# Block products in the gate stage of a three-layer float32 kernel: what the change does to the time

## The reference, cut to what matters

```python
hn = _rmsnorm(h, norm_g[i])
u = hn @ w_in[i]                       # projections, convolution branch, banded attention
...
h = h + jnp.concatenate([ya, yb], axis=-1) @ w_out[i]
e = _rmsnorm(p[i] @ w_pe[i], pe_g[i])  # 512 x 256 by 256 x 2048
h = h + e * jax.nn.sigmoid(h @ w_pg[i])
```

## Time and profile before

| | us |
|---|---|
| median of three runs (2524.76 to 2526.66) | 2524.79 |
| profiled execution | 2524.99 |
| its span | 2523.2 |
| TensorE busy in the span | 2515.8 |
| first layer's gate stage, first to last matmul (716.8 to 890.9) | 174.1 |

### The profile page before, as it was taken

How to read it: one execution, slowest core, us unless ns; L and a number is a source line. 1 busy time by engine, 2 the same in 40 slices (tenths; PEclk the granted TensorE clock), 3 DMA queues, 4 the chain that set the end, 5 groups by cost and what they waited for, 6 DMA issues and landing times.

```text
span 2523.2 us, 40982 instructions
## 1 busy us (share of the span) xinstructions
PE 2515.8 (100%) x15264; PEld 2130.5 (84%) x15264; DVE 1549.4 (61%) x2510; ACT 1066.7 (42%) x1618; POOL 1324.5 (52%) x1668
## 2 busy tenths in 40 slices
PE   9999999999999999999999999999999999999999
PEld 7888888889988888888878899888888888899887
DVE  7977766575462387777665745634654655955722
ACT  6212365643462342223655434634322656545421
POOL 6555554443355555555454434555666776534554
PEclk9999999999999999999999999999999999999999
DMA  7322243248733333223432487233322323388322
GB/s 251 114 92 99 97 123 113 91 144 210 165 108 125 116 118 101 98 94 101 120 114 95 162 188 171 92 133 114 112 98 94 101 92 100 98 188 241 101 95 105
DMA packets 95424, 313.56 MB, mean 124 GB/s; under 512 B 9456, under 2 KB 25584, under 8 KB 92208
## 3 DMA queue, kind: packets, MB, share of 16 engines
q1 hardware_dynamic: 75264, 268.45, 31.6%
q0 software_dynamic: 10368, 37.75, 8.6%
q10 hardware_dynamic: 9648, 5.36, 1.0%
HBM read 297.86 MB, written 16.81 MB: 125 GB/s over the span
## 4 chain that ended last, share of the span: by engine, by line
PE 99%; DMA 0%; ACT 0%; DVE 0%; issue 0%; SPq 0%; POOL 0%; DVEq 0%; ACTq 0%
PE acc L2070 18%; PE acc L2071 18%; PE acc L2072 17%; PE sc L2071 6%; PE sc L2070 6%; PE sc L2072 6%; PE sc L2340 2%; PE sc L2341 2%; PE sc L2342 2%; PE acc L2340 1%; PE acc L2341 1%; PE acc L2342 1%; PE acc L2094 1%; PE sc L2094 1%; PE sc L2096 1%; PE sc L2100 1%
## 5 line engine op out<-in xcount | busy, mean ns | idle before, releaser
L792 POOL TENSOR_TENSOR WL<-raw,WH 128x256 fp32r<-128x256 f32 x1504 | 1195.0, 827 | 907.6 <-ACT WH L852 907.3
L2070 PE MATMUL acc<-XH,WH 128*128 128x512 f32 x1936 | 756.4, 391 | 0.1
L2071 PE MATMUL acc<-XL,WH 128*128 128x512 f32 x1936 | 753.7, 389 | 0.0
L2072 PE MATMUL acc<-XH,WL 128*128 128x512 f32 x1936 | 753.3, 389 | 0.0
L852 ACT ACTIVATE WH<-raw 128x1024 fp32r<-128x1024 f32 x378 | 398.9, 1058 | 795.2 <-PE acc L2072 538.6
L2070 PEld LDWEIGHTS acc<-XH,WH 128*128 128x128 f32 x1936 | 363.4, 188 | 80.5 <-issue 4.9
L2072 PEld LDWEIGHTS acc<-XH,WL 128*128 128x128 f32 x1936 | 363.5, 188 | 76.0
L2071 PEld LDWEIGHTS acc<-XL,WH 128*128 128x128 f32 x1936 | 363.5, 188 | 74.3
L2070 PE MATMUL sc<-XH,WH 128*128 128x512 f32 x640 | 249.0, 389 | 0.0
L2071 PE MATMUL sc<-XL,WH 128*128 128x512 f32 x640 | 249.0, 389 | 0.0
L2072 PE MATMUL sc<-XH,WL 128*128 128x512 f32 x640 | 249.0, 389 | 0.0
(11 more groups left out here) (425 smaller groups left out, 4408.3 us busy)
## 6 DMA issues: line engine op xcount, KB each, us to landing
raw<-in_w SPq DMA_DIRECT2D x416, 512.0 KB, 3.3
raw<-in_w POOLq DMA_DIRECT2D x54, 512.0 KB, 6.2
a<-in_w POOLq DMA_DIRECT2D x18, 512.0 KB, 5.9
a<-in_w SPq DMA_DIRECT2D x16, 512.0 KB, 7.6
h_spill<-H SPq DMA_DIRECT2D x8, 1024.0 KB, 6.1
H<-h_spill SPq DMA_DIRECT2D x8, 1024.0 KB, 8.2
a<-bias_band SPq DMA_DIRECT2D x16, 384.0 KB, 3.7
H<-in_x SPq DMA_DIRECT2D x5, 1024.0 KB, 7.6
```

The source lines that it names most:

```text
L792: part = pool.tensor_tensor(WL[:, c], raw[:, c], WH[:, c].bitcast(F), ALU.subtract)
L2070: pe.matmul(bank, WH[:, c], xh, start=first, stop=False)
L2071: pe.matmul(bank, WH[:, c], xl, start=False, stop=False)
L2072: return pe.matmul(bank, WL[:, c], xh, start=False, stop=last)
```

## The change

The gate stage of both layers now runs its 16 tiles as P_PLAIN = 6 plain tiles (0 to 3, 14 and 15) and P_PAIRS = 5 pairs of tiles (4 to 13) as block products, 35 in each layer, in the order `P_STEPS`.

- **Plain tiles** alternate between the two banks G; `halve` is gone, ScalarE takes the tanh from the bank (or from T for the tiles of pairs) with scale 0.5.
- **Sums of h** for the block products are made at the stage's start: `sum_adds`, `third_add`, `sum_highs`, `third_high`, `sum_lows`, `third_low`, and `sums_of(4)` during the last plain unit. They need the room of Y, so e is stored to DRAM (`e_spill`, four parts), and comes back tile by tile (`e_load`) into `acc` and `rs`, the last two tiles into Y.
- **Weights of the block products** have five places: the four slots of `raw` and the fourth slot of WL (`wa2`). Low parts therefore rotate through three slots of WL (`p_low_slot`); high parts keep four. The chain p1, p5, p6, p4 of a pair uses one of three places `wa`, and p2, p3, p7 share one of two places `wd`.
- **Low parts** of p2 and p7 (all but the first, nine in a layer) are made by GpSimd, the others by VectorE, at most two products ahead (`block_lows(j + 2)` in turn j; three ahead in the stages of before).
- **Results** go to T (`block_outs`); a finished tile is then gated, squared and summed, in turns set by `g_done(n)`.
- **Stores** of h: tiles 0 to 3 go out before the block products, the other twelve, 256 KB each, during the next stage's first units.
- At the next stage TensorE starts its pair of tiles after the products that held its banks.

```diff
+P_PLAIN = 6
+P_PAIRS = 5
+P_STEPS = (
+    ("p2", 0), ("p1", 0), ("p5", 0), ("p3", 0), ("p1", 1), ("p6", 0), ("p2", 1), ("p7", 0), ("p5", 1), ("p4", 0), ("p3", 1), ("p6", 1),
+    ("p1", 2), ("p7", 1), ("p2", 2), ("p5", 2), ("p4", 1), ("p3", 2), ("p6", 2),
+    ("p1", 3), ("p7", 2), ("p2", 3), ("p4", 2), ("p5", 3), ("p1", 4),
+    ("p3", 3), ("p6", 3), ("p5", 4), ("p3", 4), ("p7", 3), ("p6", 4), ("p4", 3), ("p7", 4), ("p2", 4), ("p4", 4))
+def p_slot(j):
+    return (j + (j >= 14)) % RING
+def p_low_slot(j):
+    return RING - 1 if j == P_N - 1 else (j + 2) % (RING - 1)
+def p_place(kind, q):
+    if kind in ("p1", "p5", "p6", "p4"):
+        return "wa%d" % ((q + 1) % 3)
+    return "wd%d" % ((q + 1) % 2 if (kind, q) == ("p2", P_PAIRS - 1) else q % 2)
...
@@ GpSimd
+                for j, (kind, q) in enumerate(P_STEPS):
+                    name = p_place(kind, q)
+                    if j in P_SIDE:
+                        pool.wait_ge(fast_high, fast_base(ly) + j + 1)
+                        pool.wait_ge(*p_wl_free(ly, j))
+                        for k in range(LOW_PARTS):
...
+                            part = pool.tensor_tensor(WL[:, to], P_PLACE[name][:, lo:hi], WH[:, high].bitcast(F), ALU.subtract)
+                        part.then_inc(side_low, 1)
+                    if p_next(j) is not None and not p_loads(p_next(j)):
+                        pool.wait_ge(*p_low_made(ly, j))
+                        pool.dma_start(P_PLACE[name], w[p_unit(ly, *P_STEPS[p_next(j)])], accum_op=ALU.add).then_inc(w_added_in[name], 16)
@@ ScalarE, end of the plain tiles and the block products
+                square(3)
+                block_prep(1)
+                gate(4)
+                act.wait_ge(w_used, u0 + PG0 + P_U - 1)
...
+                block_prep(2)
+                square(4)
+                gate(5)
+                for j in range(3, P_N + RING):
+                    for n in SPLITS:
+                        if j == g_done(n) + 6:
+                            square(n)
+                        if j == g_done(n) + 4:
+                            gate(n)
+                    if j < P_N:
+                        block_prep(j)
+                    else:
+                        act.wait_ge(fast_used, pg0 + j - RING + 1)
+                        prep(u0, PG0 + 2 * RING + j - P_N)
+                    if 4 <= j < 6:
+                        third_high(j - 2)
+                    if j == 5:
+                        square(5)
...
@@ VectorE, the block products
+                for j in range(P_N):
+                    for n in SPLITS:
+                        if j == g_done(n) + 4:
+                            sums(n)
+                    if j - 2 == P_LATE:
+                        block_outs(j - 2)
+                    if j and j - 1 != P_LATE:
+                        block_outs(j - 1)
+                    if j + 2 < P_N and not p_close(j + 2):
+                        block_lows(j + 2)
+                    if j == 0:
+                        scaled(5)
+                        gated(5)
+                    if 2 <= j < 4:
+                        third_low(j)
+                    if 1 <= j < 3:
+                        third_add(j + 1)
+                    if j == 3:
+                        sums(5)
...                     (gated(n) in turn g_done(n) + 2, scaled(n) in turn g_done(n) + 1)
+                    if j + 2 < P_N and p_close(j + 2):
+                        block_lows(j + 2)
+                    if j >= P_N - 2:
+                        for k in range(2):
+                            next_low(2 * (j - P_N + 2) + k)
+                block_outs(P_N - 1)
+                sums(NT - 3)
+                scaled(NT - 1)
+                next_low(4)
...
@@ TensorE
-                quad_tile(n0 + N_PG, u0 + PG0, 0, x0 + 2 * NT)
-                quad_tile(n0 + N_PG, u0 + PG0, 1)
...
-                quads(n0 + N_PG, u0 + PG0, 1)
+                for t in range(P_PLAIN):
+                    if t >= 2:
+                        pe.wait_ge(g_th, ly * NT + t - 1)
+                    unit(u0 + (PG0 + 2 * t), 2 * t % RING, 0, G[t % 2], None if t else x0 + 2 * NT)
+                    unit(u0 + (PG0 + 2 * t + 1), (2 * t + 1) % RING, 1, G[t % 2], None if t else x0 + 2 * NT)
...
+                for j, (kind, q) in enumerate(P_STEPS):
+                    bank = XB_OF[bank_of(kind, q)][:, 0:HALF]
+                    back = p_last(j, lambda i: bank_of(*P_STEPS[i]))
+                    pe.wait_ge(*p_low_made(ly, j))
+                    if back is not None:
+                        pe.wait_ge(fast_out, fast_base(ly) + back + 1)
...
```

More of the change, by code:

```diff
@@ L184 @@
 W_ORDER = sorted(((q, row) for q in range(W_PAIRS) for row in range(2)), key=lambda i: w_done(*i))
+P_PLAIN = 6
+P_PAIRS = 5
+P_U = 2 * P_PLAIN
+P_SKIP = 4 * P_PAIRS
+P_STEPS = (
[4 rows of a table added]
+P_N = len(P_STEPS)
+P_AT = {step: j for j, step in enumerate(P_STEPS)}
+P_SIDE = [j for j, (kind, _) in enumerate(P_STEPS) if j and kind in ("p2", "p7")]
+P_SIDES = len(P_SIDE)
+P_LOWS = [1, 0] + [j for j in range(2, P_N) if j not in P_SIDE]
+P_LATE = P_AT["p1", P_PAIRS - 1]
+assert P_N == len(P_AT) == 7 * P_PAIRS
+assert P_PLAIN + 2 * P_PAIRS == NT and P_U == PG_U
@@ new lines, in p_close, with p_first, p_loads, p_count @@
+def p_close(j):
+    return any(p_place(*P_STEPS[i]) == p_place(*P_STEPS[j]) for i in range(max(0, j - 3), j))
+def p_first(j):
+    return all(p_place(*P_STEPS[i]) != p_place(*P_STEPS[j]) for i in range(j))
+def p_loads(j):
+    return P_STEPS[j][0] in ("p1", "p2", "p3")
+def p_count(name, loads, n=P_N):
+    return sum(p_place(*P_STEPS[i]) == name and p_loads(i) == loads for i in range(n))
+def p_rows_before(j, part):
+    kind, q = P_STEPS[j]
+    return max((i for i in range(j) if P_STEPS[i][1] == q and part in rows_of(P_STEPS[i][0])), default=None)
@@ new lines, in p_done, with g_tile, g_place @@
+def p_done(q, row):
+    return max(P_AT[kind, q] for kind in (("p5", "p3", "p6", "p7") if row else ("p1", "p2", "p4")))
+P_ORDER = sorted(((q, row) for q in range(P_PAIRS) for row in range(2)), key=lambda i: p_done(*i))
+def g_tile(n):
+    if n < PLAIN:
+        return n
+    return n + NT - P_PLAIN if n < P_PLAIN else PLAIN + 2 * P_ORDER[n - P_PLAIN][0] + P_ORDER[n - P_PLAIN][1]
+def g_place(n):
+    return n % 4 if n < P_PLAIN else 2 * ((P_ORDER[n - P_PLAIN][0] + 1) % 2) + P_ORDER[n - P_PLAIN][1]
@@ L187, with g_done, place_before @@
+def g_done(n):
+    return p_done(*P_ORDER[n - P_PLAIN])
+def place_before(n):
+    return max(i for i in range(n) if g_place(i) == g_place(n))
+SPLITS = range(P_PLAIN, NT)
+TAIL_N = NT - 2
 BLOCKS = (1, 2, 0, 3)
@@ new lines, in _ @@
+                first_load(("p1", 2))
+                first_load(("p2", 1))
+                sp.wait_ge(sum_tail, 16 * ly + parts_begun(4))
+                e_load(1)
+                first_load(("p2", 0))
+                e_load(2)
+                first_load(("p1", 0))
+                e_load(3)
+                e_load(4)
+                for n in range(3):
+                    h_store(n)
+                e_load(5)
+                h_store(3)
+                skip += P_SKIP
+                kept = 7 if ly == DEPTH - 1 else 5
@@ L743, in _ @@
+                for k in range(RING):
+                    sp.wait_ge(wl_ready, u0 + (LAYER_U + k + 1))
+                    load(u0 + (LAYER_U + RING + k + skip), k)
+                    for n in range(PLAIN + 3 * k, PLAIN + 3 * k + 3):
+                        h_store(n)
+            skip = DEPTH * (SKIP_U + P_SKIP)
             units(B0, 4, RG0 - RING - B0, skip=skip)
@@ L1153, in xc_high @@
+                for t in range(UT, NT):
+                    if t == UT + 2:
+                        square(NT - 1)
+                    xhigh(t, tl(H, t), norm_col(ly + 1, t))
             def xc_high(g):
@@ L1740, in _ @@
                 gated(1)
[L1741 to L1763 removed]
+                sums(0)
@@ new lines, in _ @@
+                sums(1)
+                scaled(2)
+                gated(2)
+                sums(2)
+                scaled(3)
+                gated(3)
+                sums(3)
+                scaled(4)
+                gated(4)
+                block_lows(1)
+                for c in range(4):
+                    dve.wait_ge(sum_head, s0 + 10 + c + 1)
+                    dve.tensor_tensor(sums_of(4, True)[:, 2 * c:2 * c + 2, :], fourth(c),
+                                      sums_of(4, False)[:, 2 * c:2 * c + 2, :].bitcast(F), ALU.subtract).then_inc(sum_tail, 1)
@@ L1766, in _ @@
+                block_outs(P_N - 1)
+                sums(NT - 3)
+                scaled(NT - 1)
+                next_low(4)
+                next_low(5)
+                gated(NT - 1)
+                sums(NT - 2)
+                for k in range(6, 10):
+                    next_low(k)
+                sums(NT - 1)
+                for k in range(10, NT):
+                    next_low(k)
             xb = DEPTH * 3 * NT
```

500 lines of the change are left out of this document (359 added, 141 removed).

## The result

The changed kernel takes 2532.97 us (median of 8 runs, 2530.66 to 2535.71) where the kernel before takes 2524.79 (8 runs, 2524.38 to 2527.48): ratio 1.003, 95% interval [1.0019, 1.0041]. It is slower by 0.3%. The forecast was 2517, the range 2509 to 2525: wrong in sign, and the time lies outside the range. The profiled execution of after took 2532.62 us, span 2530.8, which is 7.6 more than the span of before.

What follows compares the result with a forecast made beforehand. TensorE's own work was taken to bound the kernel. From the profiled 2524.99 us, less 16.0 saved, plus waits of 2.1 and 3.3 (start), 0.6 (middle) and 1.8 (end), came 2516.8, forecast as 2517, range 2509 to 2525.

Steps and rivals of the forecast that it cites:

- The saving: TensorE, gate stage: ten plain tiles out (108.8 us), 35 block products in (100.8), 8.0 us saved per layer, 16.0 in two.
- Costed at nothing: Gate stage: sums of h, two banks for four, store and loads of e, and later stores of h cost no time.
- The start: First block products: TensorE waits at products 5, 6 and 7, 2.1 us in the first layer, 3.3 in the second.
- gated(4) to -7.6, low part to -6.4: Before the last plain unit's end (0): VectorE finishes gated(4) 7.6 us and the next low part 6.4 us earlier.
- The second layer's extra: Second layer's gate stage: second squares and sums add waits, 3.3 for 2.1 at the start, 1.0 for 0.5 at the end.
- The middle: Block products around 13, 14, 20 and 21: some landings late, 0.3 us taken in each layer.
- The end: Next stage's first units wait for low parts, and low parts of h follow: 0.5 us first layer, 1.3 second.
- Landings of 7 us: Rival, weights' adding DMAs: 1.2 us more per landing, 4.4 to 5 us in all, time 2522; chance 0.18.
- VectorE through the port: Rival: GpSimd's nine low parts a layer each hold up VectorE's by 2.0 to 2.6 us, about 2525; chance 0.10.
- The first pair's wait in every pair: Rival: queues behind one another in ScalarE's and VectorE's orders repeat the wait at all five pairs, 2538; chance 0.10.
- The saving whole: Rival: margins remove most waits at the block products, so the full saving stays, 2509 to 2513; chance 0.26.
- 0.12 for slower: Whole kernel: chance 0.12 that it measures slower, beside 0.66 for faster (below 2519.9) and 0.22 for within.

Runs made afterwards that it cites:

- kernel 7: Changed kernel with e loads first, low parts 1, 2 and 5 earlier, and ScalarE's next-stage high parts first: 2514.75 us, 0.9960 of before.
- experiment 1: Changed kernel with SyncE's loads of e for tiles 2 and 3 ahead of two first weight loads: 2526.16 us, 0.9997 of before.
- experiment 9: kernel 7 with the two weight loads put back ahead of the loads of e: 2524.87 us, 1.0003 of before.
- experiment 4: Changed kernel with both the earlier loads of e and low part 1 ahead of the fifth tile's gate work: 2521.76 us, 0.9987 of before.
- experiment 5: experiment 4 with VectorE's low part 2 ahead of the sixth tile's gate work and low part 5 earlier: 2517.60 us, 0.9965 of before.
- experiment 8: kernel 7 with the first four stores of h put later, one each in turns 9 to 12: 2517.92 us, 0.9969 of before.
- experiment 2: Changed kernel with VectorE's low part 1 ahead of the gate's fifth tile: 2530.99 us, 1.0025 of before.
- experiment 11: kernel 7 with low part 2 back behind the sixth tile's gate work, low part 5 left early: 2518.36 us, 0.9974 of before.
- experiment 3: Changed kernel with unused filler matmuls on TensorE before product 0, ten and seventeen by layer: 2533.0 us, 1.0028 of before.
- experiment 6: experiment 4 with ScalarE's high parts of the next stage's first four units ahead of squares and gates: 2523.14 us, 0.9988 of before.

## Why the prediction was wrong

**The saving, 16.0 us: right.** 227 and 120 ns stand in after, and in kernel 7 the sum closes with this term.

**"Costed at nothing": here it failed.** The sentence on the loads of e said that they "run where DMA is at 35%" and that "if one is late it is VectorE that waits, not TensorE at once". I asked whether the transfer would be slow, and it was not; I did not walk SyncE's queue, where the change itself puts the third load behind a weight load whose semaphore comes 10 us later. VectorE did wait, 7.4 and 7.0 us, and TensorE not at once but at product 0 (2.4 and 4.2 us; the prediction's list of waits begins at product 5), since low parts 1 and 0 stand behind the gate work on the same engine. Experiments 1 and 9 show it from both sides: 6.8 us gained and 10.1 lost by the place of two loads. The two loads are not the whole of the 16 us between forecast and measurement: with them moved the kernel still takes 2526.16, and it needs the order of VectorE's low parts too (experiments 4 and 5, 8.6 us more) to reach the forecast time.

**The start, 2.1 and 3.3: measured 6.6 and 10.0** (up to product 7 of each layer: in the first 2.59 + 1.95 + 1.60 + 0.49, in the second 4.37 + 2.14 + 0.61 + 1.77 + 1.09; 1.6 and 2.1 of this are slow clock). The step that failed is its first line, "gated(4) to -7.6, low part to -6.4": it let VectorE be idle then, and every load of e and of weights be there. In after low part 1 ended at -1.0, and even with two loads of e moved at -4.2 (experiment 1). The walk from low part 1 to low part 5 was sound, as experiment 4 shows in the first layer. A second error stands beside this one: I placed the gate stage of before at 716.8, while the embedding product ahead of it ends, and the stage begins, at 711.3, and it ends at 885.8, so that the window had the right length and lay 5 us late. Read so, VectorE's gate work seemed to come 5 us sooner after the stage's start than it does; no run shows what this did to the forecast.

**The second layer's extra, 1.7 in the forecast (1.2 at the start, 0.5 at the end):** in experiment 4 it is 7.5. The sixth tile's gate work stands between high part 2 and low part 2 (1652.8 to 1656.8, the second sum's 0.7 us in it, which I had counted at product 5 only), the landing ahead of it took 1.8 us more than in the first layer, and 1.6 us of slow clock followed the wait. Experiment 5 takes 7.1 of the layer's 10.4 away.

**The middle, 0.3 each: measured 1.3 and 0.4.** The walk had the right place, products 20 and 21 (0.47 and 0.41); the rest is a wait of 0.6 before product 11 in the first layer, at which I had none. **The end, 0.5 and 1.3: measured 0.7 in the first layer, and in the second 1.4 and 0.6** for a low part of h, where I had 1.0 and 0.3. That it is so near is in part luck, since a late start hides some of it: once the start is in time, in experiment 5, the end takes 0.8 and 2.3, and 0.7 for the low part of h.

**The rivals.** *Landings of 7 us*: the adding loads of after took 5.3, 6.5 and 8.8 us (least, median, most; line L1098), between forecast and rival; one long landing made product 2 of the second layer late in experiment 4, so this rival had a part; with low part 2 first, no gain shows from a landing shorter by 1.6 (experiment 8). *VectorE through the port*: in after two low parts of VectorE met GpSimd's, one in each layer, and TensorE waited at none of the four products behind them. VectorE's first, then GpSimd's:

```profile
800.76 3.67 DVE L2104 TENSOR_TENSOR WL<-WA,WH 128x1024 fp32r<-128x1024 f32 x1
...
1683.13 4.19 DVE L2104 TENSOR_TENSOR WL<-WA,WH 128x1024 fp32r<-128x1024 f32 x1
```
```profile
1680.35 5.87 POOL L1093 TENSOR_TENSOR WL<-raw,WH 128x256 fp32r<-128x256 f32 x8
```

The second ended at 1687.32, 1.1 us after the last of GpSimd's eight parts (1686.22); the first likewise, at 804.43 after 803.34. The Trainium skill, "SBUF — State Buffer", "Who interferes with whom", has the engine that comes second wait for the whole of the other's instruction. By that, as an estimate, each would have taken 2 us at most (0.73 for one part and its own 1.22); these rows show it waiting 2.6 and 3.1 us, through three and a half and four parts in a row. *The first pair's wait in every pair*: no; from product 7 on the two layers together have 1.7 us of excess before the end. It was the right kind of mechanism, one queue behind another, at the wrong place: I looked for it in ScalarE's and VectorE's orders and not in SyncE's. *The saving whole*, 2509 to 2513: kernel 7 comes to within 2 us of it, by order alone.

**The chances.** 0.12 for slower was too little for a change that hands the order of four queues over in a new form. The rivals shared one blind spot: none followed SyncE's queue, and all took low part 1 to be in time.

## What to carry to other kernels

Where the profile of before has hardly a wait, what a change saves in matmuls can be read from it, as here, and what it puts in front of other work cannot: walk every queue that it rewrites from its first instruction, the queue that issues the loads above all, and ask of each entry when the one ahead of it is released. An entry that waits long holds back all behind it, however short their transfers. Then look at lists with a late item behind independent work (a low part behind a gate, a high part behind a square): here four edits of order turned +8 us into -10. And a wait's price is read by removing the chain's first late link; here removing a later one, or the slow clock behind it, mostly moved the wait. A total that meets the forecast proves little by itself: lay its terms side by side, as in experiment 4.

## What the runs showed of the hardware

TensorE's clock fell to 1.2 GHz in the middle of a kernel that runs at 2.4 otherwise: for 6.8 us, beginning within the wait, at waits of 4.2 (after), 4.6 (experiment 2) and 4.5 (experiment 9); for 3.4 us after, among others, waits of 2.4 and 1.8 (after), 2.8 (experiment 2), 2.3 (experiment 1), 1.8 (experiment 4) and 1.9 (experiment 11). After others as long it did not: 2.9 (experiment 9, first layer), 2.5 (experiment 3), 2.0 (experiment 6, second layer) and 3.1 (experiment 1, end of the second layer). In these runs it cost time only where nothing else was late: taking it out of the block products gained nothing in experiment 3, and it cost 2.4 us in experiment 9. The first matmul after a wait was 0.1 us longer than its kind (0.39 for 0.28). A low part of VectorE that meets a run of GpSimd's ended 1.1 us after the last of them, in before as in after (1.22 us became 3.25, 3.67 and 4.19).
